# Constant products on TensorE around the norms of two stacked two-layer networks

## The reference

```python
def _modulate(x, shift, scale):                 # norms "m": before a mixer or an FFN
    return _layernorm(x) * (1.0 + scale) + shift
def _post(x, f, gate, g, b):                    # norms "p": after it
    return _layernorm(ALPHA * x + gate * f, g, b)
for l in range(DEPTH):                          # first_block; shift, scale, gate come from c @ w_ada[l]
    ...
    x = _post(x, _latent_mixer(_modulate(x, sh1, sc1), mem, cos, sin, p), g1, ln1_g[l], ln1_b[l])
    x = _post(x, _ffn(_modulate(x, sh2, sc2), p), g2, ln2_g[l], ln2_b[l])
for l in range(DEPTH):                          # second_block
    h = rms_norm(x, attn_pre_norm[l])
    mix = hybrid_mixer(h, ...)
    x = x + rms_norm(mix, attn_post_norm[l])
    h = rms_norm(x, ffn_pre_norm[l])
    x = x + rms_norm(conv_ffn(h, w_up[l], conv_w[l], conv_b[l], w_down[l]), ffn_post_norm[l])
```

## Time and profile before

| | |
|---|---|
| three runs | 3074.21, 3079.66, 3084.74 us; median 3079.66 |
| the profiled execution | 3080.42 us, its span 3078.6 us |
| TensorE | matmuls busy 93% of the span, weight loads 79% |
| VectorE, ScalarE, GpSimd | 42%, 43%, 45% |
| DMA | 359 MB, queue busy 36% of 16 engines |
| mean granted TensorE clock | 0.953 of full speed |
| chain that ended last | PE 82%, DVE 9%, ACT 6%, POOL 1%, waits on nothing seen 1%, DMA 1% |

### The profile page before, as it was taken

One profiled execution on the slowest core, in us unless ns is written; L12 is line 12 of the kernel. 1 busy time (PEld: TensorE's weight loads), 2 busy tenths in 40 slices (PEclk: granted clock), 3 DMA queues, 4 the chain that ended last, 5 costly groups with the idle time before them and its releaser, 6 DMA issues.

```text
span 3078.6 us, 44754 instructions
## 1 busy us (share of the span) xinstructions
PE 2848.4 (93%) x18684; PEld 2439.6 (79%) x18684; DVE 1297.2 (42%) x2725; ACT 1323.7 (43%) x2220; POOL 1379.8 (45%) x646
## 2 busy tenths in 40 slices
PE   7999997899998999998999899899898899898898
PEld 5777876688875888877778699889886799777897
DVE  2757867532334111014467664232236441164440
ACT  3254443323424322225454346444455464444563
POOL 3331020244432543435432177578652488532686
PEclk8999999999998999998999999899899899898899
DMA  6332021133324343334311154355443255431354
GB/s 231 117 104 79 28 76 62 55 117 96 117 82 168 116 144 118 120 117 166 91 55 42 42 160 149 117 158 179 143 131 110 83 183 170 126 121 62 132 178 126
DMA packets 103552, 359.45 MB, mean 117 GB/s; under 512 B 11126, under 2 KB 17526, under 8 KB 102840
## 3 DMA queue, kind: packets, MB, share of 16 engines
q1 hardware_dynamic: 103352, 356.60, 36.4%
HBM read 355.51 MB, written 1.05 MB: 116 GB/s over the span
## 4 chain that ended last, share of the span: by engine, by line
PE 82%; DVE 9%; ACT 6%; POOL 1%; issue 1%; DMA 1%; SPq 0%; DVEq 0%; ACTq 0%
PE PS L357 82%; ACT AR L1128 1%; DVE AR L1748 1%; POOL RINGL L2465 1%; ACT WH L1108 1%; ACT XT L1128 1%; DVE XT L1748 1%; DVE ARR L1748 1%; PE PS L360 1%; DVE AR L1756 1%; DVE PS L1756 1%; DVE SM L1984 1%; ACT L1128 1%; DVE AR L1909 1%; DVE HT L1748 1%
## 5 line engine op out<-in xcount | busy, mean ns | idle before, releaser
L2465 POOL TENSOR_TENSOR RINGL<-RING,WH 128x1024 fp32r<-128x1024 f32 (+1 forms) x554 | 1298.9, 2356 | 1582.8 <-ACT WH L1108 1582.4
L357 PE MATMUL PS<-HTR,WH 128*128 128x256 f32 (+2 forms) x2736 | 884.9, 324 | 0.0
L1108 ACT ACTIVATE WH<-RING 128x1024 fp32r<-128x1024 f32 (+1 forms) x554 | 568.2, 1034 | 666.1 <-PE PS L357 535.4
L357 PE MATMUL PS<-HTH,WH 128*128 128x256 f32 (+1 forms) x2336 | 754.1, 324 | 32.5 <-POOL RINGL L2465 22.4
L357 PE MATMUL PS<-HTH,RINGL 128*128 128x256 f32 (+1 forms) x2336 | 724.3, 316 | 0.2 <-POOL RINGL L2465 0.2
L357 PE MATMUL PS<-ARR,WH 128*128 128x256 f32 (+2 forms) x2688 | 698.1, 327 | 26.1 <-ACT WH L1108 5.8
L357 PEld LDWEIGHTS PS<-HTR,WH 128*128 128x128 f32 (+1 forms) x2736 | 531.3, 194 | 40.9 <-issue 2.6
L357 PEld LDWEIGHTS PS<-ARR,WH 128*128 128x128 f32 (+1 forms) x2688 | 472.2, 193 | 74.1 <-issue 17.6
L357 PEld LDWEIGHTS PS<-HTH,WH 128*128 128x128 f32 x2336 | 453.1, 194 | 75.1 <-issue 36.9
L357 PE MATMUL PS<-ARR,RINGL 128*128 128x256 f32 (+1 forms) x1472 | 467.0, 327 | 0.0
L357 PEld LDWEIGHTS PS<-HTH,RINGL 128*128 128x128 f32 x2336 | 443.7, 192 | 28.5 <-POOL RINGL L2465 0.4
(11 more groups left out here) (192 smaller groups left out, 3333.8 us busy)
## 6 DMA issues: line engine op xcount, KB each, us to landing
RING<-w_ada_in SPq DMA_DIRECT2D x96, 512.0 KB, 3.7
RING<-w_up_in SPq DMA_DIRECT2D x88, 512.0 KB, 3.3
RING<-w_gates_in SPq DMA_DIRECT2D x48, 512.0 KB, 3.6
RING<-w_ff_gate_in SPq DMA_DIRECT2D x44, 512.0 KB, 3.7
RING<-w_ff_up_in SPq DMA_DIRECT2D x44, 512.0 KB, 3.7
RING<-w_glu_in SPq DMA_DIRECT2D x32, 512.0 KB, 4.5
RING<-w_ff_down_in SPq DMA_DIRECT2D x32, 512.0 KB, 3.6
RING<-w_in_in SPq DMA_DIRECT2D x32, 512.0 KB, 3.7
```

The source lines that it names most:

```text
L357: return e.matmul(out_, lhsT, rhs, start=start, stop=stop)
L1108: e.activation(RINGS[name][:, j, 0:width], RING[:, b % NSLOT, 0:width], ACT.Copy).then_inc(*a_upper.up(b))
L2465: e.tensor_tensor(RINGL[:, i, 0:width], RING[:, i, 0:width], RINGS[name][:, j, 0:width], ALU.subtract).then_inc(*g_lower.up(b))
```

## The change

A helper `warm(n)` puts n products ONES x M1024 (float32, 128x128 by 128 columns, start and stop set) into the bank that the next `take` will hand out, after the wait that this `take` would do anyway. Nothing reads them. `warm` stands in `layernorm`: before each of the eight tiles of the means (norms "m" but the first), after the mean's spread (5), before tiles 2, 4 and 6 of var (2 at 512 columns, 1 at 256), after var (5), and behind rstd of the norms "m" but the first (10 or 7); 18 stand behind the first norm's `fill_all`. In `normed`: 6 at its start, 3 before each tile from the second on (1 in the first), 4 behind the sum, 8 or 6 behind rrstd. In `mix_scale`: 6 at its start. Nothing is taken away or moved.

```diff
--- before.py
+++ after.py
@@ -356,6 +356,14 @@
             def mm(out_, lhsT, rhs, start, stop):
                 return e.matmul(out_, lhsT, rhs, start=start, stop=stop)
 
+            def warm(n):
+
+                i = turn[0] % in_turn[0]
+                if i in held:
+                    pe.wait_ge(*held[i][0].to(*held[i][1:]))
+                for _ in range(n):
+                    mm(banks[i][:, 0:128], ONES, M1024, True, True)
+
             def turned(out_, in_, n):
                 return e.transpose(out_, in_, IDENT[0:n, 0:n])
 
@@ -491,6 +499,8 @@
                 n = cols.stop - cols.start
                 o = take("means", *nid, until=(a_norm, "mean", *nid))
                 for k in range(8):
+                    if nid[0] == "m" and nid[1:] != (0, 1):
+                        warm(1)
                     ready(k)
                     t = in_strips(o, src[:, k, cols], k == 0, k == 7)
                 t.then_inc(*p_norm.up("means", *nid))
@@ -499,14 +509,20 @@
                 pe.wait_ge(*a_norm.to("mean", *nid))
                 out_of_strips(o, MEAN, n).then_inc(*p_norm.up("mean", *nid))
                 fill(1)
+                warm(5)
                 o = take("var", *nid, until=(a_norm, "sd", *nid))
                 for k in range(8):
+                    if k in (2, 4, 6):
+                        warm(2 if n == 512 else 1)
                     pe.wait_ge(*a_norm.to("sq", *nid, k // 2))
                     t = in_strips(o, SQN[:, k, 0:n], k == 0, k == 7)
                 t.then_inc(*p_norm.up("var", *nid))
+                warm(5)
                 o = take("rstd", *nid, until=(d_norm, "mul", *nid, 7))
                 pe.wait_ge(*d_norm.to("rstd", *nid))
                 out_of_strips(o, RSTD, n).then_inc(*p_norm.up("rstd", *nid))
+                if nid[0] == "m" and nid[1:] != (0, 1):
+                    warm(10 if nid == ("m", 0, 2) else 7)
 
             def gla_gates(l, seq, tile):
                 for d in range(2):
@@ -803,6 +819,7 @@
                     fill_all()
                     ring("WH0")
                     ada_at[:] = 4, 4, 12
+                    warm(18)
                 h0 = lambda k: g_norm.to("lo", *part(("m", l, 1), k, 0 if l else 1))
                 h1 = lambda k: g_norm.to("lo", "m", l, 1, k)
                 halves = [("w_glu", i % 2 * 8 + i // 2, (a_merge if i % 2 else d_merge, "glu", l, i // 2))
@@ -862,13 +879,18 @@
 
             def normed(nid, ready):
                 o = take("rms", *nid, until=(a_norm, "rsd", *nid))
+                warm(6)
                 for k in range(8):
+                    if k:
+                        warm(1 if nid == (0, 1) else 3)
                     pe.wait_ge(*a_norm.to("rsq", *nid, k))
                     t = in_strips(o, view({1: 14336, 2: 18432}[nid[1]], 8, 256)[:, k, :], k == 0, k == 7)
                 t.then_inc(*p_norm.up("rms", *nid))
+                warm(4)
                 o = take("rrstd", *nid, until=(d_norm, "nmul", *nid, 7))
                 pe.wait_ge(*d_norm.to("rrstd", *nid))
                 out_of_strips(o, RSTD, 256).then_inc(*p_norm.up("rrstd", *nid))
+                warm(8 if nid[1] == 1 else 6)
 
             def projections2(l, h):
                 project_tok("w_t1", l, 0, range(2), 284, 2, HN, h, lambda t: (d_mix, "t1", l, t))
```

## The result

The changed kernel takes 3088.19 us (median of 20 runs, 3079.34 to 3098.88); the kernel before, beside it on the same chip, 3079.12 us (20 runs). The ratio is 1.0028, 95% interval 1.0018 to 1.0037: 8.6 us slower. The forecast was 14 us less. The profiled execution took 3085.81 us, its span 3084.0 us.

What follows compares the result with a forecast made beforehand. TensorE was taken to set the time, about 290 us of it at half speed, 173 at the norms. Costs of 14.3, gains of 29.1 and 1 for remaining drops made -14 us from 3080.4: 3066 predicted, range 3052 to 3077.

Steps and rivals of the forecast that it cites:

- the price of one product: Everywhere products are added: 0.247 us each at full clock, from 14 records in 1.73 us; 0.51 as the bound for cold.
- Point 1: Vars of the norms, where TensorE had no pause: added products cost 6.6 us, 2.7 of it at `("p",0,1)`.
- Point 2: Means of `("m",1,1)`, 64 records in one run: 8 products, some cold, cost 2.1 us.
- Point 3: Sums in `normed`: tiles 0.92 us apart instead of 0.72 cost 3.9 us at three places, 1.5 at `normed((0,1))`.
- Point 4: Before rstd: 5 products (1.24 us) against a pause of 1.02 to 1.65 cost 0.2 us.
- Points 5 to 8: At the norms: spreads 10.6, first matmuls 12.9, `w_ada` pieces 2.7 and 1.5, shorter ends of sums 1.4; gains 29.1 us.
- Point 5: Spreads at half clock: 0.85 us comes back from each of about 12.5, 10.6 us gained.
- Point 6: First matmuls behind a norm run at full clock instead of half: 12.9 us gained.
- Pieces run into each other: Rival: products dense where TensorE had no pause, partly cold; gain about 4 us, 3076, no measurable change; chance 0.20.
- The clock still falls: Rival, all loops over tiles: products don't hold the clock, each costs 0.51; about 75 us slower, 3155; chance 0.06.

Runs made afterwards that it cites:

- Kernel 4: Changed kernel with one product wherever a loop had two or three (var at 512 columns, three of the four `normed`): 3076.65 us, ratio 0.9990.
- kernel 9: Changed kernel with all 347 products in place, each with 32 columns of ONES instead of 128: 3061.31 us, ratio 0.9937.
- blocks alone: Also kernel 1: changed kernel without the 133 products inside the loops over tiles, the 214 in blocks kept: 3061.42 us, ratio 0.9935.
- Kernel 3: Changed kernel without the products in two loops, the means of `("m",1,1)` and the sum of `normed((0,1))`: 3074.05 us, ratio 0.9983.
- kernel 7: The blocks alone without the blocks behind the last spread of each norm, all other blocks kept: 3063.19 us, ratio 0.9939.
- kernel 2: Changed kernel with only the products inside the loops over tiles, all other `warm` calls removed: 3123.09 us, ratio 1.0143.
- kernel 5: The blocks alone plus 16 products in the pause of 4.49 us before the means of `("m",1,1)`: 3056.44 us, ratio 0.9916.
- kernels 8: The blocks alone, same places and number, each product with 32 columns of ONES instead of 128: 3060.43 us, ratio 0.9931.

## Why the prediction was wrong

**The step that failed is the price of one product, as used in points 1 to 3.** It was taken from fourteen records in one run, 0.247 us each, and carried into the loops, where a product stands alone between tiles of 32 columns. There one costs 0.49 us and three cost 0.93, and at half clock one costs 0.86, where 0.51 was taken as the bound. Kernel 4 against the changed one shows the size, kernel 9 the cause: it is paid in going from 32-column tiles to a 128-column weight block and back, for with 32 columns it is gone, while in a run by themselves both widths cost the same. By the traces the eight places add 28.8 - 12.5 = 16.3 us to the forecast and the attentions' clock 5.3. The runs of 57 and 64 records in the earlier trace rows were so dense because their form didn't change on the way; the prediction read their density as "no pause, so each product adds itself", and left out the change of form.

**Point 1** (vars, 6.6 us): var of `("p",0,1)` lost 2.0, with 2.7 forecast; the block of five in it cost nothing (blocks alone: 0.0), so the six in the loop cost 2.0, and not 1.5. `("p",0,2)` lost 4.1 with 1.2 forecast; 1.9 of it are waits for the DMA of `w_ada`, in the timeline of PE of the changed kernel:

```profile
1385.33 1.05 PE L357 MATMUL PS<-RING,SCP 128*32 128x512 f32 x4 [0.72 <-DMA RING<-w_ada_in]
1387.74 1.05 PE L357 MATMUL PS<-RING,SCP 128*32 128x512 f32 x4 [1.36 <-DMA RING<-w_ada_in]
```

The kernel before had one wait of 0.21 us there. Kernel 3 has both, kernels 1, 4 and 9 don't; why they come is open. `("m",0,2)` lost 3.4, with 1.1 forecast: the last piece of `w_ada` came 0.54 us late from DMA, the squares were ready by then, and all its pairs of tiles ran one behind the other, 1.22 us each.

**Point 2** (means of `("m",1,1)`, 2.1 us) cost 7.8: one product with its switches, at half clock, adds 1.32 - 3.64/8 = 0.86 us to each tile. The prediction had said that nothing fills the pause before it, and had made the products cold in part, but had no price for the switch, and the switch too was paid at half clock.

**Point 3** (`normed`, 5.4 us): 2.6 + 2.1 + 2.1 + 4.7 = 11.5. The tiles were 1.11 us apart, and 0.92 forecast; the loop of (0,1) was cold as a whole.

**Point 4** (0.2 us) was right within what the table can tell: with the blocks alone the lag doesn't grow at any of the eight places (0.0 to -0.9 us).

**Points 5 to 8, the gains,** held as a sum. The blocks alone gain 20 us although their clock falls in some loops. In the changed kernel the end lies at +5.4, the eight places give 28.8 and the attentions, in which nothing was changed, 5.3 (from -3.7 to +1.6); the rest is 28.8 + 5.3 - 5.4 = 28.7 us of gain, and 29.1 were forecast. This is a remainder and not a measurement of each point, and that it comes so near to 29.1 is in part luck. Point 5 can be read in the trace: the spreads together take 9.0 us less than before, against 10.6 forecast. At the norms two are slow still or anew, that of the mean of `("m",1,1)` (2.08 us, before 1.16) and the last of `normed((0,1))` (1.81, before 1.97). Point 6 isn't earned by the blocks that were meant to earn it, except at the first norm: kernel 7 without them gives the same time, since the blocks before already hold the clock.

**The rivals.** "Pieces run into each other" (3076) named the right places, and put 10 us on them and on point 6 together, where 16 came at the eight places alone (28.8 - 12.5). Its own condition, a seventh of the time cold, isn't what happened at three of the four `normed`, where the clock was 1.00. "The clock still falls" came true in two loops of the changed kernel, and in 8 of the 15 of kernel 2. The Trainium skill's rule (TensorE: Matmul & The Clock Gate, Terms), throttled time x (1 - K/N), would give 77 us, an estimate, for the 154 us that the clock was up longer; the traces show some 29 us of gains. The rule also counts time in which nothing waited for TensorE.

**Is the switch known?** The Trainium skill (TensorEngine Tiling (Array Packing), Key Properties) says that a change of the tiling mode, and not just of the tile, drains TensorE; it gives no time for it. The trace agrees in kind. In `normed((0,2))` of the changed kernel 0.15 us pass from the start of a tile's last record to that of the first wide product, and 0.21 us from the start of the last wide product to that of the next tile; with narrow products (kernel 9) these are 0.04 and 0.05 us. The difference, 0.27 us, is the part that experiment 4 found once per gap. That the array drains in this time is the page's word; the runs show only that the cost goes with the change of width. The page on the clock gate (of the Trainium skill too, Part 3, Packing small matmuls) says that matmuls in other tiles of the array run at the same time. A tile's eight records here take 219 to 244 ns each and all lie within 0.32 us, which agrees.

## What to carry to other kernels

- Price an instruction in the neighbourhood in which it will stand: a price from a run of equals isn't that of one between strangers. A filler should have the form of what surrounds it, here one slice made 28 us.
- Fill the pause before a dense or awaited stretch; put nothing between tiles whose inputs are ready, unless it fits the pace that another engine sets (here 0.73 us a tile, room for one wide product or just about three narrow ones).
- A higher mean clock isn't a gain: 290 us at half clock became 136, and the kernel got slower; with 146 and a third fewer products (kernel 5) it was 34 us faster than that.

## What the runs showed of the hardware

- A wide float32 product between two 32-column tiles costs 0.49 us at full clock, three cost 0.93, five in a row before a tile take 1.31; a narrow one costs about 0.2 us (pairs of tiles every 0.87 us with two, 0.49 without).
- With narrow products in place of wide ones the mean granted clock was the same: 0.972 over the span in kernels 1 and 8, 0.978 in the changed kernel and kernel 9. The prediction had set the width of the strips against the rival that the clock still falls; kernels 8 and 9 don't bear that argument out. Why the strips of the earlier trace rows, 3.64 us in one run, stay at half clock wasn't tested.
- In kernel 9 records of narrow products and of the strips stand mixed in the trace, a product among the strips of a tile:

```profile
2412.58 0.26 PE L357 MATMUL PS<-AR,CM 128*32 128x64 f32 x3
2412.64 0.27 PE L357 MATMUL PS<-CM 128*32 128x128 f32 x1
2412.66 0.37 PE L357 MATMUL PS<-AR,CM 128*32 128x64 f32 x5
2412.86 0.71 PE L357 MATMUL PS<-CM 128*32 128x128 f32 x5
```

In the changed kernel tiles and products never mix like this, and a product begins 0.25 us behind the start of the tile before it (2432.48 - 2432.23); the narrow one begins 0.14 us behind (2409.80 - 2409.66).
- With the same program between them, the attentions shifted the lag by up to 5 us from one profiled execution to the next (66.5 to 504.7 us in the table), along with the time at half clock there. Single lags are read across one place only, never over such a stretch.
- Time moves with the clock from execution to execution of one kernel too. The shortest of the 20 of the changed kernel (3079.34 us) has a mean clock of 0.980, 123 us at half clock; the longest (3098.88 us) has 0.972, 173 us: 19.5 us of time for 50 us at half clock. Around the norms it was less, 29 us for 154.
